# A mixer and mixture-of-experts step on one core: input loads, head order, output projection, router and closing stage rearranged

## The chip, the cores and the metric

The kernel runs on one core of a Trainium2 chip. A core has the matrix engine (PE, with its weight loads listed as PEld), VectorE (DVE), ScalarE (ACT), GpSimd (POOL) and SyncE (SP), and 16 DMA engines. DMAs are issued from the instruction streams of SP, ACT and POOL; the profile lists the issues as SPq, ACTq and POOLq, and the packets by queue: q1 carries what SP issues, q10 what ACT issues, q0 what POOL issues. The metric is the time of one execution in microseconds (us).

## What is computed

One layer for 288 tokens (256 of a prompt, 32 of eight decoded sequences), model width 1024, all in float32:

```
a = rms_norm(x, g_mix);  z = a @ w_in                       # 28 blocks of 128 columns, and r1 with 16
log_a = log_sigmoid(r1 @ w_gk2 + b_gk2) / 16
o1, s1 = chunk_gated_linear(q1, k1, v1, log_a, state)       # 4 heads; chunks of 64 tokens
o2, s2 = chunk_gated_linear(silu(q2), 1-f, silu(i2), log f) # 4 heads
h = x + concat(head_norm(o1)*silu(g1), head_norm(o2)*sigmoid(g2)) @ w_out
logits = rms_norm(h, g_ffn) @ w_router + b_router           # 32 experts, top 4, softmax of the 4
h += sum over the 4 experts of gate * (swiglu(xn @ w_gu[e] + b_gu[e]) @ w_dn[e] + b_dn[e])
h += sigmoid(rms_norm(h, g_ple) @ w_ple_gate) * (p @ w_ple_proj)
y = rms_norm(h, g_final);  outputs: y and the four new states
```

Every expert is computed for up to 64 tokens (its slots); the weights of an expert are 12 MB, of all 32 together 403 MB.

## The kernel before

Activations stand transposed in SBUF: `hT`, `aT` and `acc` are [128, 8, 288], eight chunks of 128 features by 288 tokens. The program is written out by hand for each engine, with semaphores between them; each engine runs its own list in order, and so does each issuing queue.

**Front.** ACT issues `x_prompt` in one DMA and `x_sample`, eight small rows of vectors (L624), `r1w`, `gk2`, `w_rt`, `b_rt`, `p_tok` and `w_pp` before its first copy (L637). PE turns x over (24 transposes, L844) chunk by chunk into PSUM, ACT and DVE copy the even and the odd chunks to `hT`, and DVE multiplies with `g_mix` into `acc`. PE waits for all eight copies, then projects four column blocks from `acc` (the scale 1/rms is applied afterwards); after the first it sums the squares with eight matmuls against `ones`, and between the third and the fourth it computes r1 with eight matmuls of 16 columns out of `aT`. Blocks 4 to 19 follow in a loop, at eight matmuls of 128x128 by 288 each.

**Heads stage.** The last eight column blocks (`project_late`) stand between the parts of the recurrence. Heads go out through PSUM banks `O_BANK`; after heads 0 and 1 come blocks 6 and 7, then heads 2 to 5, the sums of squares of heads 0 to 3 (`head_sums(0)`), heads 6 and 7 and `head_sums(1)`. ACT turns the sums into 1/rms by Ln and Exp (`heads_rinv`), DVE norms each head (`head_norm`, two instructions).

**Output projection.** Eight chunks of `w_out` (512 KB each) go through the same four `wst` slots as `w_in`. Chunks 0 to 3 are computed with heads 0 to 3 first, and then with heads 4 to 7; chunks 4 to 7 follow, each with `stream_chunk(c - 4)`, two accumulating matmuls of 32 columns for the sum of squares and the router's logits. All of the DMAs of `w_out` are on SP, chunks 4 to 7 each after `h_done` of the chunk whose slot they take and ahead of one unit of expert weights.

**Expert weights.** 384 units of 1 MB (`UNITS` = 12 for each expert, eight of `w_gu` with rows of 8 KB and four of `w_dn` with rows of 4 KB) go through 14 slots: 12 of the ring, `vmask` (V_SLOT) and `acc` (A_SLOT). The ring's memory holds the mixer's arrays before. SP issues the first unit after `o_ready` 8 and the first `h_done`, the unit of A_SLOT after `h_done` 8, and every later one when PE has used the unit that held its slot (`u_used`, L516).

**Router.** After the stream chunks PE turns all of `aT` back to rows (24 transposes), then the logits, already multiplied with 1/rms, and the column of 1/rms. DVE finds the top four, counts membership (`memb`), PE ranks tokens within experts by matmuls with a triangle, and turns the gates (`gateT`); DVE builds the one-hot `sel` for four experts at once.

**First expert.** PE gathers the chosen tokens with matmuls of `tok` by `sel`: four chunks, `bias(0)`, then `gate_up` of two chunks, two gathers, `gate_up` of two, two gathers and the rest. One `gate_up` uses one unit in four matmuls of 64 columns by 512, in pairs that share the array.

**Closing stage.** PE computes the per-layer gate in eight chunks (L1302 on), DVE and ACT finish each chunk: scale, sigmoid, multiply, add to `hT`, multiply with `g_final` (`finish`, one chunk behind), squares and their sum (`add_square`); PE turns the finished chunks to rows (`final_chunk`), sums squares to a column (`final_sums`), and the results are scaled and stored.

## Time and profile before

| | us |
|---|---|
| median of three runs | 1249.48 (1248.81 to 1252.28) |
| the profiled execution's own time | 1253.93 |
| span of its trace | 1252.2 |
| PE busy | 1189.8 (95%) |
| DVE busy | 270.5 |
| ACT busy | 183.4 |
| bytes moved | 437.61 MB, mean 349 GB/s |

Times in the trace are counted from the first instruction of the span. A PE that is busy need not be at its peak, and the trace gives the clock that it was granted for each stretch, as a share of full speed.

### The profile page before, as it was taken

The page shows a single profiled execution, that of the slowest core. Times are in us where ns is not written, and L with a number is a line of the kernel's source. Part 1 is how long each engine was busy: PE and PEld are TensorE (multiplying, and loading weights), DVE is VectorE, ACT ScalarE, POOL GpSimd, SP SyncE. Part 2 cuts the span into 40 slices and gives each one's busy share as a digit, 9 for nine tenths or more (in the row PEclk, how much of TensorE's full clock was granted, in tenths as well). Part 3 has the DMA queues.
Part 4 walks back from the last instruction along what each step waited for, and adds up shares of the span by engine and source line. Part 5 has one row for each costly group of instructions (what it writes and reads, how often), then busy time and mean ns, then how long its engine had stood idle before and what let it go on. Part 6 is the DMA issues. An engine that isn't in the chain of part 4 may idle for free.

```text
span 1252.2 us, 12674 instructions
## 1 busy us (share of the span) xinstructions
PE 1189.8 (95%) x5432; PEld 567.6 (45%) x5433; DVE 270.5 (22%) x507; ACT 183.4 (15%) x310; POOL 22.4 (2%) x43
## 2 busy tenths in 40 slices
PE   7999999899999999999999999999999999999887
PEld 4777777643334444444433333333333333333355
DVE  2136733310111112211111111111111111111144
ACT  2142023211010101111110101010101111101032
POOL 3002000000000000000000000000000000000000
PEclk9999979899999999999999999999999999999998
DMA  7462654989999999999999999999999999999931
GB/s 186 118 168 68 163 153 157 380 308 415 418 412 418 417 417 418 417 417 416 418 417 418 417 417 417 416 417 418 417 417 418 417 416 417 417 417 417 417 152 38
DMA packets 127744, 437.61 MB, mean 349 GB/s; under 512 B 9708, under 2 KB 59976, under 8 KB 94888
## 3 DMA queue, kind: packets, MB, share of 16 engines
q1 hardware_dynamic: 123872, 433.22, 87.4%
q10 hardware_dynamic: 3544, 3.30, 0.9%
q8 instruction: 43, 0.70, 0.2%
q0 software_dynamic: 272, 0.28, 0.1%
q14 instruction: 13, 0.11, 0.0%
HBM read 432.04 MB, written 4.72 MB: 349 GB/s over the span
## 4 chain that ended last, share of the span: by engine, by line
PE 51%; DMA 39%; SPq 4%; DVE 3%; ACT 1%; ACTq 1%; issue 1%; DVEq 0%
PE ps L834 49%; DMA ring<-in_w_gu 35%; SPq L516 4%; DMA vmask<-in_w_gu 2%; DMA acc<-in_w_gu 2%; PE ps L1187 1%; ACTq L629 0%; DVE ring L1395 0%; PE ps L1209 0%; ACTq L624 0%; PE ps L1073 0%; DVE wst L1635 0%; DVE wst L1632 0%; DVE ring L1480 0%; PE ps L1291 0%
## 5 line engine op out<-in xcount | busy, mean ns | idle before, releaser
L834 PE MATMUL ps<-ring,s 128*64 128x512 f32 x960 | 215.4, 595 | 13.6 <-DMA ring<-in_w_gu 13.4
L834 PE MATMUL ps<-ring,wst 128*64 128x512 f32 x912 | 207.3, 598 | 2.0 <-ACT wst L769 2.0
L834 PE MATMUL ps<-ring,aT 128*64 128x512 f32 x832 | 187.2, 595 | 7.7 <-DMA ring<-in_w_gu 7.5
L1628 DVE TENSOR_SCALAR wst<-ps 128x512 f32<-128x512 f32 x32 | 22.1, 691 | 741.3 <-PE ps L834 741.3
L834 PEld LDWEIGHTS ps<-ring,s 128*64 128x64 f32 x960 | 66.1, 137 | 160.1 <-issue 115.3
L834 PEld LDWEIGHTS ps<-ring,aT 128*64 128x64 f32 x832 | 57.8, 137 | 131.9 <-issue 104.9
L834 PEld LDWEIGHTS ps<-ring,wst 128*64 128x64 f32 x912 | 61.0, 136 | 115.8 <-issue 112.4
L834 PE MATMUL ps<-aT,wst 128*128 128x288 f32 x384 | 95.1, 408 | 3.0 <-ACT ring L669 3.0
L834 PE MATMUL ps<-sel,tok 128*128 128x256 f32 x384 | 95.4, 388 | 1.2 <-DVE sel L1590 1.2
L767 ACT ACTIVATE wst<-wst 128x512 f32<-128x512 f32 x32 | 20.1, 630 | 506.7 <-DVE wst L1628 506.7
L834 PEld LDWEIGHTS ps<-aT,wst 128*128 128x128 f32 x384 | 72.3, 190 | 25.1 <-ACT ring L669 3.4
L834 PEld LDWEIGHTS ps<-sel,tok 128*128 128x128 f32 x384 | 71.7, 194 | 15.3 <-issue 4.0
L834 PE MATMUL ps<-selT,wst 128*128 128x288 f32 x256 | 72.2, 421 | 2.4 <-issue 1.8
L834 PE MATMUL ps<-acc,wst 128*128 128x288 f32 (+1 forms) x240 | 61.6, 455 | 2.7 <-DVE acc L1507 1.5
L834 PEld LDWEIGHTS ps<-selT,wst 128*128 128x128 f32 x256 | 45.6, 189 | 39.7 <-issue 28.6
L834 PE MATMUL ps<-bgu,ehot 128*64 128x512 f32 x256 | 60.4, 592 | 0.0
L759 ACT COPY wst<-ps 64x512 f32<-64x512 f32 x63 | 36.5, 579 | 128.3 <-PE ps L834 127.5
L834 PEld LDWEIGHTS ps<-acc,wst 128*128 128x128 f32 (+1 forms) x240 | 40.7, 185 | 22.2 <-issue 8.7
L834 PEld LDWEIGHTS ps<-bgu,ehot 128*64 128x64 f32 x256 | 18.3, 137 | 36.3 <-issue 36.3
L834 PE MATMUL ps<-aT,ring 128*128 128x288 f32 x128 | 32.2, 406 | 0.0
L769 ACT COPY wst<-ps 128x512 f32<-128x512 f32 x32 | 18.7, 585 | 84.9 <-PE ps L1187 84.9
L834 PE MATMUL ps<-vmask,aT 128*64 128x512 f32 x112 | 26.6, 595 | 1.1 <-DMA vmask<-in_w_gu 1.1
(253 smaller groups left out, 725.8 us busy)
## 6 DMA issues: line engine op xcount, KB each, us to landing
ring<-in_w_gu SPq DMA_DIRECT2D x224, 1024.0 KB, 20.6
ring<-in_w_dn SPq DMA_DIRECT2D x114, 1024.0 KB, 24.2
vmask<-in_w_gu SPq DMA_DIRECT2D x20, 1024.0 KB, 21.1
wst<-in_w_in SPq DMA_DIRECT2D x28, 512.0 KB, 3.9
acc<-in_w_gu SPq DMA_DIRECT2D x12, 1024.0 KB, 18.1
vmask<-in_w_dn SPq DMA_DIRECT2D x8, 1024.0 KB, 26.0
acc<-in_w_dn SPq DMA_DIRECT2D x6, 1024.0 KB, 23.1
wst<-in_w_out SPq DMA_DIRECT2D x8, 512.0 KB, 3.7
```

The lines of the kernel that those rows point to most:

```text
L516: sp.dma_start(as_unit(weights(e, c), c), unit_src(e, c)).then_inc(u_loaded[slot_of[u]], 16)
L759: act.copy(to[:, half * BANK:(half + 1) * BANK], ps[half * SLOTS:(half + 1) * SLOTS, 5, :]).then_inc(yr_copied, 1)
L767: act.activation(sbuf, gbuf, ACT.Sigmoid, scale=SWIGLU_ALPHA).then_inc(sigm_ready, 1)
L769: act.copy(hidT, ps[:, 3, :]).then_inc(hT_copied, 1)
L834: return pe.matmul(o, lhsT, rhs, start=start, stop=stop, skip_group_check=True)
L1187: ins = pe.transpose(ps[:, 3, c * P:(c + 1) * P], ubuf[:, c * P:(c + 1) * P], ident[:])
L1628: dve.tensor_scalar(gbuf, ps[:, 0, :], SWIGLU_LIMIT, None, ALU.min).then_inc(gate_ready, 1)
```

## The change

x comes in three loads: its first 128 rows on SP ahead of the weights, the second 128 and `x_sample` on ACT. The loads of `r1w`, `gk2`, `w_rt`, `b_rt`, `p_tok` and `w_pp` stand later in ACT's list. PE starts with eight matmuls of the identity, DVE multiplies straight from PSUM, ACT copies all of `hT`, and the squares are summed on DVE so that PE needs one matmul. r1 is computed in four column groups of 32. Heads alternate with the late blocks. The projection of chunk 0 waits head by head. The `w_out` chunks 4 to 7 are issued by ACT, SP starts the expert weights from `su_done` 3 and `o_done` 8 on in another order of slots. Rows are turned back chunk by chunk, the router's logits are multiplied with 1/rms after they are turned, `bias(0)` stands before the ranks, `sel` of the first four experts is built tile by tile, the gates are turned during expert 0. In the closing stage each chunk is finished at once.

```diff
-        queue = [(i, None) for i in range(UNITS + 2)]
+        queue = [(i, None) for i in (V_SLOT, 8, 9, 10, 11, 6, 7, 0, 1, 2, 3, 4, 5, A_SLOT)]
...
+            sp.dma_start(tok[:, 0, :], io["x_prompt"][0, 0:P, :]).then_inc(x0_loaded, 16)
             for i in range(LATE + G):
                 load_cols(i)
...
             sp.wait_ge(su_done, 3)
-            sp.wait_ge(o_ready, HEADS)
-            sp.wait_ge(sp_stored, 16 * 2)
-            sp.wait_ge(s0_stored, 16 * KU)
-            for c in range(UNITS):
-                if c < KD - WSLOTS:
-                    load_cols(NZ + WSLOTS + c)
-                sp.dma_start(unit_dst(c), unit_src(0, c)).then_inc(u_loaded[slot_of[c]], 16)
+            for u in range(UNITS + 2):
                 e, c = u // UNITS, u % UNITS
+                if u == 1:
+                    sp.wait_ge(o_done, HEADS)
+                    sp.wait_ge(sp_stored, 16 * 2)
+                if slot_of[u] == 6:
+                    sp.wait_ge(s0_stored, 16 * KU)
+                if slot_of[u] == 0:
+                    sp.wait_ge(o_ready, HEADS)
+                if slot_of[u] == A_SLOT:
+                    sp.wait_ge(h_done, KD)
+                sp.dma_start(as_unit(weights(e, c), c), unit_src(e, c)).then_inc(u_loaded[slot_of[u]], 16)
...
+            for c in range(KD):
+                act.wait_ge(xg0_ready, c + 1)
+                act.copy(hT[:, c, :], ps[:, c, 0:T]).then_inc(xT_copied, 1)
+                if c == 0:
+                    act.wait_ge(gk2_zeroed, 2)
+                    act.dma_start(r1w[:, :, 0:RANK], io["w_in"][0, :, c_r1:c_r1 + RANK].rearrange("(c p) n -> p c n", p=P)) \
+                        .then_inc(r1w_loaded, 16)
+            for j in range(4):
+                act.dma_start(gk2[j * 32:j * 32 + RANK, :], io["w_gk2"][0]).then_inc(r1w_loaded, 16)
...
+            for c in (0, 4):
+                act.activation(squares[:, c:c + 4, :], hT[:, c:c + 4, :], ACT.Square).then_inc(sq_ready, 1)
+            act.dma_start(w_rt[:], io["w_router"][0].rearrange("(c p) n -> p c n", p=P)).then_inc(small_loaded, 16)
+            act.dma_start(b_rt[:], io["b_router"][0:1, :].to_broadcast([P, E])).then_inc(small_loaded, 16)
...
             for c in range(KD):
                 act.wait_ge(h_ready, c + 1)
                 act.activation(squares[:, c, :], hT[:, c, :], ACT.Square).then_inc(sq_ready, 1)
+                if c + WSLOTS < KD:
+                    act.wait_ge(h_done, c + 1)
+                    act.dma_start(wst[:, (NZ + c) % WSLOTS],
+                                  io["w_out"][0, :, (c + WSLOTS) * P:(c + WSLOTS + 1) * P].rearrange("(c p) n -> p c n", p=P)) \
+                        .then_inc(w_loaded[(NZ + c) % WSLOTS], 16)
...
+            for i in range(8):
+                mm(ps[:, 0, 0:P], ident[:], ident[:], True, True)
...
-                        ins = mm(ps[0:RANK, 7, 0:T], r1w[:, c, :], aT[:, c, :], c == 0, c == KD - 1)
+                        q = slice((c % 4) * 32, (c % 4 + 1) * 32)
+                        ins = mm(ps[q, 7, 0:T], r1w[:, c, :], aT[:, c, :], c < 4, c >= 4)
...
             pe.wait_ge(smp_ready, 1)
             project_late(4, 0)
+            pe.wait_ge(smp_ready, 2)
+            two_heads(0)
             project_late(5, 1)
             pe.wait_ge(su_used, PAIRS)
             state_products(0)
+            two_heads(2)
+            project_late(6, 0)
             state_products(1)
+            two_heads(4)
             head_sums(0)
+            project_late(7, 1)
+            two_heads(6)
             head_sums(1)
...
             def project_out(c, h0, h1):
                 for h in range(h0, h1):
+                    if c == 0:
+                        pe.wait_ge(o_ready, h + 1)
...
             for c in range(4, KD):
                 pe.wait_ge(w_loaded[(NZ + c) % WSLOTS], 16 * (NG + 2))
-                pe.wait_ge(h_ready, c - 3)
+                pe.wait_ge(h_ready, c - 3 if c < 6 else c - 1)
                 project_out(c, 0, HEADS).then_inc(h_done, 1)
-                stream_chunk(c - 4)
+                chunks = range(0 if c == 4 else c - 1, c)
+                for k in chunks:
+                    stream_chunk(k)
+                for k in chunks:
+                    for t in range(TT):
+                        rows_chunk(k, t)
...
+            bias(0)
             pe.wait_ge(memb_ready, 1)
...
-            for c in range(4):
+            for c in range(2):
                 gather_chunk(0, c)
...
-                    if e == 0 and c in (1, 3):
-                        gather_chunk(0, c + 3)
-                        gather_chunk(0, c + 4)
+                    if e == 0 and c in (0, 1, 3):
+                        for k in (2, 3) if c == 0 else (4, 5) if c == 1 else (6, 7):
+                            gather_chunk(0, k)
...
             for c in range(KD):
                 dve.wait_ge(pg_done, c + 1)
                 dve.tensor_tensor(pgt[:, c % 2], ps[:, P_BANK[c], 0:T], rinv[:], ALU.mult).then_inc(pg_scaled, 1)
-                if c:
-                    finish(c - 1)
-                if c > 2:
-                    add_square(c - 2)
-            finish(KD - 1)
-            add_square(KD - 2)
+                if 2 <= c < KD - 1:
+                    add_square(c - 1)
+                finish(c)
```

## Rows read from the trace of the kernel before

**Rows 1.** The page: GB/s moved by DMA, the span in 40 slices of 31.3 us.

```profile
GB/s 186 118 168 68 163 153 157 380 308 415 418 412 418 417 417 418 417 417 416 418 417 418 417 417 417 416 417 418 417 417 418 417 416 417 417 417 417 417 152 38
```

**Rows 2.** Windows: length, PE, PEld, DVE, ACT, POOL busy, clock, DMA share, GB/s.

```profile
250.00:255.00 5.00, 5.00 (x24) 1.90 (x21) 0.00 (x0) 0.00 (x0) 0.00 (x0) 1.00 0.26 74
600.00:1150.00 550.00, 525.57 (x2371) 205.85 (x2367) 80.52 (x133) 58.05 (x103) 0.00 (x0) 1.00 1.02 417
```

**Rows 3.** Timeline (start, us, what): first gather, first down unit, last gate unit.

```profile
241.38 7.57 PE L834 MATMUL ps<-sel,tok 128*128 128x256 f32 x24 [1.19 <-DVE sel L1590]
...
248.88 1.94 PE L834 MATMUL ps<-bgu,ehot 128*64 128x512 f32 x8
...
275.15 0.20 PEld L834 LDWEIGHTS ps<-ring,wst 128*64 128x64 f32 x4 [0.33 <-issue]
...
1184.36 0.20 PEld L834 LDWEIGHTS ps<-ring,s 128*64 128x64 f32 x4 [1.44 <-DMA ring<-in_w_gu]
```

**Rows 4.** Timeline of the front.

```profile
7.01 5.27 ACTq L629 DMA_DIRECT2D b_rt<-in_b_router  x1
...
7.98 6.92 PE L844 MATMUL ps<-ident,tok 128*128 128x128 f32 x24 [7.98 <-DMA tok<-in_x_sample]
...
16.45 6.11 PE L834 MATMUL ps<-acc,wst 128*128 128x288 f32 x16 [1.28 <-ACT hT L637]
...
34.13 4.05 PE L834 MATMUL ps<-aT,r1w 128*16 128x288 f32 x16
...
43.36 17.00 PE L834 MATMUL ps<-aT,wst 128*128 128x288 f32 x69
```

**Rows 5.** Queues from 5 to 6 us: packets, MB, share of 16 engines.

```profile
q10 hardware_dynamic: 88, 0.36, 88.0%
q1 hardware_dynamic: 90, 0.05, 15.4%
```

**Rows 6.** Queue q1 from 7 to 8 us, and from 212 to 214 us.

```profile
q1 hardware_dynamic: 490, 0.24, 115.4%
...
q1 hardware_dynamic: 129, 0.82, 100.0%
```

**Rows 7.** Heads stage: the timeline of SP and PE, and one window.

```profile
176.63 3.92 SPq L490 DMA_DIRECT2D out<-ring  x4
...
182.59 4.19 PE L834 MATMUL ps<-ring,ones 128*128 128x288 f32 x8
...
190.74 2.19 PE L834 MATMUL ps<-ring,ones 128*128 128x288 f32 x8
...
175.00:177.00 2.00, 2.00 (x9) 1.05 (x5) 1.08 (x2) 0.00 (x0) 0.00 (x0) 0.50 0.00 0
```

**Rows 8.** Timeline of the output projection and its first and last addition.

```profile
194.38 19.67 PE L834 MATMUL ps<-acc,wst 128*128 128x288 f32 x80 [1.46 <-DVE acc L1507]
...
204.45 0.45 DVE L1537 TENSOR_TENSOR hT<-hT,ps 128x288 f32<-128x288 f32 x1 [3.86 <-PE ps L834]
...
223.96 4.15 PE L834 MATMUL ps<-acc,wst 128*128 128x288 f32 x16
...
228.14 0.45 DVE L1537 TENSOR_TENSOR hT<-hT,ps 128x288 f32<-128x288 f32 x1 [3.83 <-PE ps L834]
```

**Rows 9.** Timeline of the router, and the clock in one window of it.

```profile
236.01 0.80 DVE L1565 TENSOR_REDUCE memb<-selg 128x96 f32<-128x384 f32 x1
...
240.00:245.00 5.00, 3.81 (x11) 2.99 (x11) 2.19 (x5) 0.39 (x1) 0.00 (x0) 0.50 1.03 419
```

**Rows 10.** Timeline of the end: last chunk scaled, last sum, its Ln.

```profile
1240.04 0.46 DVE L1715 TENSOR_TENSOR wst<-ps,rinv 128x288 f32<-128x288 f32 x1 [2.02 <-PE ps L834]
...
1243.90 1.42 PE L834 MATMUL ps<-ones,tok 128*128 128x1 f32 x12 [1.65 <-DVE tok L1710]
...
1245.36 0.26 ACT L814 ACTIVATE rcol<-ps,eps 128x2 f32<-128x2 f32 x1 [0.59 <-PE ps L834]
```

**Rows 11.** The page: DMA issues of w_out, count, KB, median us from issue to landing.

```profile
wst<-in_w_out SPq DMA_DIRECT2D x8, 512.0 KB, 3.7
```

More of the change, by code:

```diff
@@ L181, in build @@
         reset = sb("reset", [P, T])
+        lgs = reset[0:E, :]
         maskf = ring[:, BLOCKS * SLOTS:BLOCKS * SLOTS + P + 32]
@@ L445, in _ @@
             cols = [(io["w_in"], c0 + j * P) for c0 in group_cols for j in range(G)]
-            cols += [(io["w_out"], j * P) for j in range(KD)]
+            cols += [(io["w_out"], j * P) for j in range(WSLOTS)]
             def load_cols(i):
@@ L550, in _ @@
             lk.add(pool.memset(ones[:], 1.0))
+            lk.wait()
+            pool.affine_select(out=ident[:], in_=ident[:], compare_op=ALU.not_equal, fill=1.0, base=0,
+                               pattern=[[-1, P]], channel_multiplier=1).then_inc(consts_ready, 1)
+            pool.affine_select(out=upper[:], in_=ones[:], compare_op=ALU.is_gt, fill=0.0, base=0,
+                               pattern=[[1, P]], channel_multiplier=-1).then_inc(consts_ready, 1)
+            pool.memset(gk2[:], 0.0).then_inc(gk2_zeroed, 1)
+            pool.memset(r1w[:], 0.0).then_inc(gk2_zeroed, 1)
             lk.add(pool.memset(reset[:], 1.0))
@@ L1087, in _, with bias @@
-            rinv_columns(1)
+            pe.wait_ge(rinv_ready, 2)
+            for t, (t0, n) in enumerate(tiles):
+                ins = pe.transpose(ps[0:n, 0, t * P:t * P + E], rinv[0:E, t0:t0 + n], ident[0:E, 0:E])
+            ins.then_inc(rc_done, 1)
+            def bias(e):
+                pe.wait_ge(ehot_ready, e + 1)
+                for b in range(2):
+                    halves(b, ehot[:], bgu[:, b * FF:b * FF + BANK], bgu[:, b * FF + BANK:(b + 1) * FF], True, False)
+            pe.wait_ge(bdn_loaded, 16)
@@ L1149, in combine_half @@
                         ins.then_inc(cb_done, 1)
-            def bias(e):
-                pe.wait_ge(ehot_ready, e + 1)
-                for b in range(2):
-                    halves(b, ehot[:], bgu[:, b * FF:b * FF + BANK], bgu[:, b * FF + BANK:(b + 1) * FF], True, False)
             def gate_up(e, c):
@@ L1571, in _ @@
             lk.add(dve.tensor_tensor(pk[:], pk[:], psum_k[:, :, 1:2].to_broadcast([P, NT, TOPK]), ALU.mult))
+            dve.wait_ge(rank_done, 1)
+            for t, (t0, n) in enumerate(tiles):
+                lk.add(dve.scalar_tensor_tensor(rankp[0:n, t, :], ps[0:n, RANK_BANK, t * E:(t + 1) * E], 1.0, memb[0:n, t, :],
+                                                ALU.add, ALU.mult))
             lk.wait()
+            for t in range(NT):
+                dve.tensor_tensor(sel[:, t], iota1[:, 0:SLOTS].unsqueeze(1).to_broadcast([P, QUAD, SLOTS]),
+                                  rankp[:, t, 0:QUAD].unsqueeze(2).to_broadcast([P, QUAD, SLOTS]),
+                                  ALU.is_equal).then_inc(sel_ready, 1)
+            lk.add(dve.tensor_copy(cnt_f[:, 0:E], ps[0:1, RANK_BANK, NT * E:(NT + 1) * E]))
+            lk.wait()
+            lk.add(dve.tensor_reduce(cnt_f[:, E:E + 1], cnt_f[:, 0:E], AX_X, ALU.max))
+            lk.wait()
+            dve.tensor_copy(cnt_i[:], cnt_f[:]).then_inc(cnt_ready, 1)
             lk.add(dve.tensor_tensor(gated.rearrange("p t k e -> p (t k) e"), onehot.rearrange("p t k e -> p (t k) e"),
```

338 lines of the change are left out of this document (162 added, 176 removed).

## The prediction

> **What bounds the kernel now.** I read the row of GB/s on the page first: from slice 10 to slice 38 it stands at 417 or so [rows 1], and the windows say the same for 600 to 1150 us, while PE is busy for 525.57 of those 550 us [rows 2]. One unit of 1.0486 MB at 417 GB/s is 2.51 us, an expert of twelve 30.2 us; PE needs 30.2 x 525.57/550 = 28.8 us for one. So DMA sets the pace of the expert stage, and at its end PE waits for the last gate unit of expert 31, at 1184.4 [rows 3]. From there to the end of the span are 67.8 us.
>
> Then I asked when that stream began to run without a gap. In 250 to 255 it moves only 74 GB/s [rows 2]: all 14 slots are full and wait for PE's first use. A unit 14 places later can be issued only when PE lets a slot go. The first gate unit is let go about 252.6 (the bias matmuls end at 250.8 [rows 3], and it takes 1.8 us itself), the first down unit, number 8, about 277.1. Counting 2.51 us a place, these ask for a stream that starts at 252.6 and at 277.1 - 8 x 2.51 = 257.0; later units ask for less, as PE gains 1.4 us an expert. The reader is to see that the time when PE uses **the first down unit** (275.15 [rows 3]) moves the end one to one, that loading the first 14 units sooner by itself moves nothing, and that beyond it only the closing stage counts.
>
> **Front.** PE is in the loop at 43.36 and started its first projection at 16.45, for ACT's copies; ACT came to them only after its DMA issues, b_rt's alone 5.27 us [rows 4]. With x and the vectors first I put the start at 12: PE had all of x at 7.98 and took 6.92 us for its 24 transposes [rows 4]; a third of them now run before the last load, and the copies no longer follow them. Bounds 9 and 16.4. That is -4.4. Summing the squares takes eight matmuls as r1 does, 4.05 us [rows 4]; one is left, 0.5: -3.5. r1 in four column groups runs two rounds of 0.5 in place of 4.05: -3.0, bound -2.0. PE then waits for the squares' sum and the norm, which come from ACT and DVE, some 0.9; if b_rt's issue holds ACT again for 5.27, up to 4.6. The queue is emptier by then, as r1w is long through, so I take 0.9. **Front: -10.0**, bounds -6.3 and -13. The Trainium skill ("TensorE: Matmul & The Clock Gate", Part 3, Measured speedup vs the span model) gives three column tiles a speedup of 2.38, not four; by that r1 would take 1.7 us and the sum be 0.7 us smaller. No row of this kernel shows four groups.
>
> **Heads.** PE does the same work in another order. From 175 to 177 the granted clock was 0.50, the level of 1.2 GHz, and the same four sums took 4.19 us there and 2.19 later [rows 7]; that level lasted from 174 to 187, and the work in it took 5.1 us more than its like elsewhere. PE was not idle; thin matmuls in a row came before it. With a 3.9 us block between every two heads I expect the clock to hold: -5.1, bound 0. The norms of heads 0 to 3 are made while block 7 and heads 6, 7 run, so the wait of 1.46 [rows 8] goes, and 1.5 us of small gaps. **Heads: -8.1**, bounds -3 and -8.1. The projection starts at 194.4 - 18.1 = 176.3; its first half costs 7.7 us, heads 4 to 7 are normed in time to within 0.2, so the first addition is at 186.3 for 204.45 [rows 8].
>
> **The w_out loads of chunks 4 to 7.** This is the step that decides. They are now issued by ACT (q10) while SP's expert weights fill q1. Two queues at once took turns: 88 packets of 4 KB in q10 and 90 of 512 bytes in q1 in the same us [rows 5], one for one, whatever their size; a pair takes an engine 16/88 = 0.18 us. A w_out load is 1024 packets of 512 bytes, 64 an engine. A packet of w_gu has 8 KB: some 98 in 2 us (0.80 of the 0.82 MB) [rows 6], 0.32 us each, so a pair is 0.335. SP gets to the weights thus: the w_out load of chunk 3 waits for block 7 and, with the four stores of states behind it (3.9 us of issues [rows 7]), is issued from 171 to 175. 2.6 MB in 512-byte packets at 0.24 MB a us [rows 6] would last to 183; I take 182. Chunk 4's load starts at 188.6 (addition 0.45, square 0.44, issue, and 1.5 us to the first byte: the 0.37 MB of 250 to 255 [rows 2] are 0.9 us of flow, after a release at 252.6). Of the eight w_gu units 2.6 are through, 5.4 are left: 43 packets an engine. Chunk 4 takes 43 x 0.335 + 21 x 0.18 = 18.2 us, landing at 207. Chunk 5 pairs with 43 packets of w_dn (7.8), with the 8 of unit 12 (2.7), and goes alone for the rest: about 217.7. Chunks 6 and 7 follow at 2.2 us each, since unit 13 waits for `h_done` 8. PE was through with chunk 3 at 191.9, so it stands for 15 us; then chunk 4 at a fallen clock 5.7 (16 records took 6.11 at the start [rows 4], 4.15 later [rows 8]), streams and transposes 3, a wait to 217.7, chunks of 3.9 with 0.75 between. The last addition comes at 230.9 for 228.14 [rows 8]: **+20.9**, and what front and heads won is gone. From below the loads cost about 4 (the shorter pair for a queue nearly empty), from above they end when q1 runs dry, near 213 for chunk 4. The Trainium skill ("DMA: Bandwidth & Descriptors", Queues, rings and completion order) says that an engine drains a packet of some 9 to 17 descriptors from one queue before it turns to the next; by that chunk 4 would need 4 to 7 turns and as many descriptors of the weights, the same within 2 us. Its section Issuing engines are not separate DMA queues says that a second issuer saves only issue time, which speaks against this part.
>
> **Router.** Stream chunks 4 to 6 and 16 row transposes are done before the last addition, the logits don't wait for 1/rms: lg_done 3.1 earlier against the last addition. `memb` by two additions saves 0.25 of the 0.80 [rows 9], the per-tile `sel` 0.6, the gates' transposes leave the path, but `bias(0)` and the scaling by a column cost it some 0.8. **-3.1**, bounds -1 and -5.
>
> **First expert.** The bias matmuls (1.94 [rows 3]) leave the stretch, the wait for the first copied gather costs 0.9, and gathers ran at half clock until 245 [rows 3, 9], 2 us lost; bias(0) in DVE's stretch keeps PE at work. -2.8, bounds 0 and -3.5. So the first down unit comes at 275.15 - 18.1 + 20.9 - 3.1 - 2.8 = 272.
>
> **Closing.** PE's eight chunks are as long. After the last one DVE scaled at 1240.04, then finished two chunks, and the Ln of the sums came at 1245.36 after 1.42 us of twelve records [rows 10]. Now one chunk is finished, its three sums take 0.4, but ACT loads its table after the last square: Ln at 1243.7, -1.6. The wait for the first finished chunk goes: -0.5. **-2.1**, bounds -1 and -2.5.
>
> The sum is -18.1 + 20.9 - 3.1 - 2.8 - 2.1 = -5.2: 1253.9 becomes 1248.7 for the profiled execution, 4.4 above the median of 1249.5, which becomes 1244.3.
>
> **The rivals.** (a) ACT's loads are not held up: engines read ahead, and the small packets slip in; chunk 4 costs 4 us. For it: the shares from 5 to 6 and from 7 to 8 us sum to over 100% [rows 5, 6], so packets overlap. Against it: the counts, 88 to 90. The last addition is then at 212 + 1, and the sum -5.2 - 17 = -22: 1227. (b) Nothing comes of it: the clock also falls among the new heads (+5.1), or b_rt holds ACT (+3.7), with no other change: 1249. Against it: heads are shorter stretches now. (c) Slower: PE's clock stays at 0.50 when it comes back from the 15 us without work, through chunks, streams and transposes to the gathers, as it was at 0.50 in 240 to 245 [rows 9], when DVE had kept it waiting for the router. Some 30 us of work at half speed cost 15, less 4 counted: +11, so 1255. It decides from 5.2 us lost, 10 us of work beyond what I count. Against it: the first projection, which also came after a rest, lost only 2 us to it (6.11 for 4.15 [rows 4, 8]).
>
> **How the numbers follow.** 0.3% of 1249.5 is 3.75 us, about what a measurement can tell. The main case gets 0.58, its own range 1240 to 1249 from the bounds of front, router and the first expert; (a) 0.26, and between 1223 and 1238; (b) 0.10; (c) 0.06. Faster: 0.70 of the main case, all of (a), a little of (b): 0.69. Same 0.21, slower 0.10. The range 1226 to 1250 leaves out the ends of (a), (c) and the tails, 2 in 10.
>
> **What would show it.** The loop at 33 in place of 43; clock 1.00 through the heads; PE idle for 10 us or more ahead of chunk 4 of the projection with the wait on w_out, and a landing time of some 18 us for 512 KB on ACT's queue in place of 3.7 [rows 11]; the first down unit at 272; Ln some 3.7 us after the last chunk is scaled, for 5.3. I am wrong if the wait at chunk 4 is under 6 us (rival a), or if the end does not follow the first down unit.

## The result and the profile after

The changed kernel takes 1259.26 us (median of 4, 1258.41 to 1259.78), the kernel before beside it 1250.11 us. The ratio is 1.0071, with a 95% interval of 1.0053 to 1.0088: the change makes the kernel slower by 0.7%. I had forecast 1244 and given "slower" one chance in ten. The profiled execution took 1258.41 us, with a span of 1256.6 us. Of all executions in this document one, of b_heads, is set apart as slow (1385.79 us at a mean granted clock of 0.846 for 0.989 to 0.993); it counts in no ratio.

The timeline of the changed kernel, from the loop to the last addition (start, us, what). The number behind x counts records; a matmul of the program gives two of them, of two instructions each:

```profile
34.41 2.83 PE L851 MATMUL ps<-aT,wst 128*128 128x288 f32 x11
...
179.19 15.68 PE L851 MATMUL ps<-acc,wst 128*128 128x288 f32 x64
...
189.16 0.45 DVE L1592 TENSOR_TENSOR hT<-hT,ps 128x288 f32<-128x288 f32 x1 [0.76 <-PE ps L851]
...
211.01 6.08 PE L851 MATMUL ps<-acc,wst 128*128 128x288 f32 x16 [16.14 <-DMA wst<-in_w_out]
...
223.17 4.15 PE L851 MATMUL ps<-acc,wst 128*128 128x288 f32 x16 [2.99 <-DMA wst<-in_w_out]
...
232.99 4.05 PE L851 MATMUL ps<-acc,wst 128*128 128x288 f32 x16
...
237.07 0.45 DVE L1592 TENSOR_TENSOR hT<-hT,ps 128x288 f32<-128x288 f32 x1 [4.00 <-PE ps L851]
```

PE is in the loop 8.95 us sooner than in [rows 4] and starts the out projection 15.2 us sooner than in [rows 8]. Then it stands for 16.14 us ahead of chunk 4 and for 2.99 us ahead of chunk 5, each time for a w_out load, and the last addition comes 8.9 us *later* than in [rows 8]. The cause stands in three views. First, ACT's own issues of these loads:

```profile
189.65 0.39 ACTq L750 DMA_DIRECT2D wst<-in_w_out  x1
191.52 0.38 ACTq L750 DMA_DIRECT2D wst<-in_w_out  x1
193.46 13.39 ACTq L750 DMA_DIRECT2D wst<-in_w_out  x1
206.92 11.93 ACTq L750 DMA_DIRECT2D wst<-in_w_out  x1
```

The third and fourth issue block ACT for 13.39 and 11.93 us. Second, the landing times (count, KB, median us from issue to landing), 26.2 us on ACT's queue where SP's loads of the same size take 3.8:

```profile
wst<-in_w_out SPq DMA_DIRECT2D x4, 512.0 KB, 3.8
wst<-in_w_out ACTq DMA_DIRECT2D x4, 512.0 KB, 26.2
```

Third, the two queues from 194 to 196 us (units in packets of 8 KB) and from 206 to 208 us (4 KB): packets, MB, share of 16 engines. q1 carries the expert units, q10 the w_out loads:

```profile
q1 hardware_dynamic: 97, 0.79, 92.9%
q10 hardware_dynamic: 97, 0.05, 8.2%
...
q1 hardware_dynamic: 183, 0.69, 88.1%
q10 hardware_dynamic: 184, 0.09, 16.6%
```

The counts are equal and the bytes are not: a packet of 512 bytes goes for each one of 8 or of 4 KB. In each us from 194 to 217 the two counts differ by 5 at most. While PE stands its clock falls; the first window below covers the heads, the two others the stand (the last three columns are granted clock, DMA share and GB/s):

```profile
174.00:187.00 13.00, 13.00 (x67) 10.65 (x66) 4.50 (x11) 7.65 (x10) 0.00 (x0) 1.00 0.97 313
195.00:201.00 6.00, 0.00 (x0) 0.00 (x0) 0.73 (x2) 0.00 (x0) 0.00 (x0) 0.74 1.03 419
201.00:211.00 10.00, 0.00 (x0) 0.00 (x0) 0.00 (x0) 0.44 (x1) 0.00 (x0) 0.50 1.03 394
```

So chunk 4 takes 6.08 us for 4.15. From the router to the end: the first gather, the first down unit (of `w_dn`), the last gate unit (of `w_gu`), the last combine (the sixteen records that bring the last expert's rows back to the tokens, here in two pieces), the gate chunks of the closing stage, the last chunk scaled and its Ln:

```profile
246.89 2.83 PE L851 MATMUL ps<-sel,tok 128*128 128x256 f32 x12 [1.02 <-DVE sel L1639]
...
277.99 2.37 PE L851 MATMUL ps<-ring,wst 128*64 128x512 f32 x10
...
1187.62 1.94 PE L851 MATMUL ps<-ring,s 128*64 128x512 f32 x8 [0.54 <-DMA ring<-in_w_gu]
...
1203.52 1.97 PE L851 MATMUL ps<-lnbuf,wst 128*128 128x288 f32 x7 [0.68 <-ACT wst L778]
1208.58 3.84 PE L851 MATMUL ps<-lnbuf,wst 128*128 128x288 f32 x9 [3.10 <-issue]
1212.26 4.53 PE L851 MATMUL ps<-aT,ring 128*128 128x288 f32 x18
...
1246.44 0.46 DVE L1771 TENSOR_TENSOR wst<-ps,rinv 128x288 f32<-128x288 f32 x1 [1.89 <-PE ps L851]
...
1250.15 0.26 ACT L833 ACTIVATE rcol<-ps,eps 128x2 f32<-128x2 f32 x1
```

The first down unit is 2.8 us later than in [rows 3] and the last gate unit 3.3 us: the end of the stream follows the first down unit, as the prediction's first part has it. Longer than before is the stand in the last combine, 3.10 us in which PE waits for nothing that the profile names ("issue"), and the nine records behind it are slow (3.84 us, where at full clock a record is 0.25). In the kernel before this stand is 1.75 us long and comes after twelve records:

```profile
1200.26 3.18 PE L834 MATMUL ps<-selT,wst 128*128 128x288 f32 x12 [0.68 <-ACT wst L759]
1205.19 1.13 PE L834 MATMUL ps<-selT,wst 128*128 128x288 f32 x4 [1.75 <-issue]
```

### The profile page after: what moved, and what is told of

Same layout as the page of the kernel before. It is cut to its first block, busy times and chain, and to the rows that moved or that the text cites. A ratio compares the mean times of both kernels' runs of the same rounds, so it can differ in the third digit from the quotient of the medians.

```text
span 1256.6 us, 12703 instructions
## 1 busy us (share of the span) xinstructions
PE 1183.8 (94%) x5440; PEld 564.4 (45%) x5441; DVE 273.5 (22%) x508; ACT 184.8 (15%) x314; POOL 22.9 (2%) x45
## 4 chain that ended last, share of the span: by engine, by line
PE 49%; DMA 42%; SPq 3%; DVE 3%; ACT 1%; issue 1%; ACTq 0%; DVEq 0%
PE ps L851 47%; DMA ring<-in_w_gu 35%; SPq L519 3%; DMA wst<-in_w_out 3%; DMA vmask<-in_w_gu 2%; DMA acc<-in_w_gu 2%; PE ps L1238 1%; PE ps L864 0%; DMA vec_rows<-in_gn_hgrn 0%; DVE ring L1444 0%; PE ps L1260 0%; ACTq L636 0%; DVE wst L1688 0%; DVE wst L1691 0%; DVE ring L1529 0%
## 5 line engine op out<-in xcount | busy, mean ns | idle before, releaser
L786 ACT ACTIVATE wst<-wst 128x512 f32<-128x512 f32 x32 | 20.2, 631 | 507.0 <-DVE wst L1684 507.0
L851 PEld LDWEIGHTS ps<-aT,wst 128*128 128x128 f32 x384 | 73.4, 193 | 24.6 <-ACT ring L685 3.4
L851 PE MATMUL ps<-lnbuf,wst 128*128 128x288 f32 x256 | 73.6, 428 | 3.8 <-issue 3.1
L851 PEld LDWEIGHTS ps<-sel,tok 128*128 128x128 f32 x384 | 70.1, 190 | 14.5 <-issue 5.1
L851 PEld LDWEIGHTS ps<-lnbuf,wst 128*128 128x128 f32 x256 | 46.5, 193 | 41.6 <-issue 30.0
L851 PEld LDWEIGHTS ps<-aT,ring 128*128 128x128 f32 x128 | 24.0, 190 | 6.3
## 6 DMA issues: line engine op xcount, KB each, us to landing
vmask<-in_w_gu SPq DMA_DIRECT2D x20, 1024.0 KB, 20.2
acc<-in_w_gu SPq DMA_DIRECT2D x12, 1024.0 KB, 18.2
acc<-in_w_dn SPq DMA_DIRECT2D x6, 1024.0 KB, 24.6
```

The costliest lines, as they stand in the source:

```text
L786: act.activation(sbuf, gbuf, ACT.Sigmoid, scale=SWIGLU_ALPHA).then_inc(sigm_ready, 1)
L851: return pe.matmul(o, lhsT, rhs, start=start, stop=stop, skip_group_check=True)
```

## The experiments

Every time below is a median; "ratio" is to the kernel before, run beside it, with its 95% interval.

**The kernel before, once more.** No edit.

> The kernel before, once more. Its first profiled execution took 1253.93 us, 4 us over its median, and had a half-clock stretch from 174 to 187 us in the heads; I had taken 5.1 us off for it. Theory A (that stretch is a rare guest, so its 5.1 us were never in the median): the new profile has clock 1.00 from 174 to 187, the out projection starts near 189 instead of 194.4, and the span is near 1248. Rival B (the stretch belongs to the kernel): clock 0.50 there again and the projection at 194 to 195; then the 4 us between profile and median lie elsewhere, and the heads gain of the change is real. Beside itself the kernel should come out within 0.3%, which also tells how far a comparison of this kernel can be trusted.

It took 1250.52 us beside 1248.23, ratio 1.0013 (1.0001 to 1.0026). Windows of the heads stage and of the out projection, and the projection's start:

```profile
174.00:187.00 13.00, 13.00 (x93) 10.97 (x92) 2.48 (x4) 8.10 (x13) 0.00 (x0) 1.00 0.71 203
...
200.00:240.00 40.00, 35.79 (x180) 25.14 (x179) 14.38 (x47) 9.55 (x18) 1.90 (x2) 0.92 0.98 373
...
190.97 6.33 PE L834 MATMUL ps<-acc,wst 128*128 128x288 f32 x25 [1.86 <-DVE acc L1507]
```

The clock is 1.00 from 174 to 187, the projection starts 3.4 us sooner than in [rows 8], and the span is 1248.9 us for 1252.2. Theory A holds. From the loop to the projection PE takes 146.6 us for 151.0, so the stretch at half clock cost 4.4 us and not 5.1, and it reached the loop 1 us later in this execution, so the start is 191 and not 189. The profiles of b_front, b_wout and b_pad12 below have the old order of heads too, clock 1.00 in that stage, and 145.1 to 146.7 us for the same way: one profile of five has the stretch. The mean clock of each execution goes with its time: the profiled one of the prediction had 0.988 at 1253.93 us, this one 0.993 at 1250.63; beside b_front the kernel before took 1246.58 us at 0.994 and 1254.57 at 0.986. As far as these figures tell, the spread of this kernel's times is stretches of half clock that come in some executions and not in others. The interval, just above 1 for a kernel beside itself, says that 0.1% tells nothing here.

**The w_out loads back on SP.**

```
 (SP)  for u in range(UNITS + 2):
           ...
+          if 1 <= u <= KD - WSLOTS:
+              sp.wait_ge(h_done, u)
+              sp.dma_start(wst[:, (NZ + u - 1) % WSLOTS], <w_out, chunk u + 3>)
 (ACT) -   act.wait_ge(h_done, c + 1); act.dma_start(wst[...], <w_out, chunk c + 4>)
```

> The changed kernel, but the w_out loads of chunks 4 to 7 are issued by SP again, in turn with the expert units 1 to 4, each after its h_done, as in the kernel before. Theory Q (the loads lost their time to the units queued on the other queue): chunk 4 lands some 4 to 6 us after its issue instead of 15 to 30, PE waits under 3 us ahead of chunks 4 and 5, the last addition comes near 214 instead of 237.1, the first down unit near 255 to 257, and the end follows it by 20 to 23 us: 1237 to 1240. Rival S (the stream's start sets the end, and units issued 10 us later than in the changed kernel cost it back): first down unit early, but the last gate unit not before 1180, and 1248 to 1255.

1236.47 us (1236.41 to 1236.62), ratio 0.9903 (0.9883 to 0.9923): theory Q, half a us below its range. The page gives 3.8 us to landing for all eight loads. Projection, chunk 7 of it, first down unit and last gate unit:

```profile
179.07 19.56 PE L851 MATMUL ps<-acc,wst 128*128 128x288 f32 x80
...
211.28 4.05 PE L851 MATMUL ps<-acc,wst 128*128 128x288 f32 x16
...
256.27 7.09 PE L851 MATMUL ps<-ring,wst 128*64 128x512 f32 x32
...
1165.68 1.94 PE L851 MATMUL ps<-ring,s 128*64 128x512 f32 x8 [0.55 <-DMA ring<-in_w_gu]
```

Chunk 4 follows chunk 3 without a gap. Chunk 7 starts 32.2 us after the projection did, for 53.8 in the changed kernel: the loads' place on ACT's queue costs 21.6 us there. The first down unit comes 21.7 us sooner and the span is 21.9 us shorter. The expert units from the second on start 8.5 us later here (189.46 for 180.98), and nothing is lost by it: rival S is out.

**ACT issues, but SP waits for its loads.**

```
 (SP)  if u == 1:
           ...
+          for k in range(WSLOTS):
+              sp.wait_ge(w_loaded[(NZ + k) % WSLOTS], 16 * (NG + 2))
```

> The changed kernel with ACT still issuing the w_out loads of chunks 4 to 7, but SP holds unit 1 and all later ones until those four loads have landed. Theory Q (sharing between the queues is the cost): as good as with the loads on SP, since 14 units need only 35 us and are not wanted before 252: last addition near 214, 1237 to 1240. Rival I (what costs is that ACT issues them, between its squares: 13.4 and 11.9 us of blocked issues): the issues stay long, the squares and so the streams stay late, and the time stays above 1250.

1236.68 us, ratio 0.9908 (0.9886 to 0.9929), the same as with the loads on SP. Queue q10 from 194 to 196 us, with no row of q1 in that window, and the landing time on ACT's queue:

```profile
q10 hardware_dynamic: 980, 0.49, 83.9%
...
wst<-in_w_out ACTq DMA_DIRECT2D x4, 512.0 KB, 4.1
```

The four issues take ACT 0.37 to 0.39 us each. So the blocked issues of the changed kernel were not a property of ACT; they come where its queue drains slowly (a_split below, in between, has 3.81 and 7.53 us). Rival I is out: the company on the DMA engines is the cost, not the issuer. The second unit and all behind it start at 200.27 here, 19.3 us later than in the changed kernel, and that too costs nothing.

**Smaller packets for the units.** Units 1 to 13 in four loads of 512 columns (w_dn: 256), nothing else.

```
 (SP)  for q in range(4):
           sp.dma_start(<quarter q of the unit's columns>).then_inc(u_loaded[slot_of[u]], 16)
       # waits on u_loaded of these slots: + 48
```

> The changed kernel, all its queues and its order kept; only units 1 to 13 are loaded in four parts of 512 columns each, so that their packets have 2 KB instead of 8 KB or 4 KB. Theory Q1 (packets are taken one for one from the two queues, whatever their size): a pair of packets then moves 2.5 KB instead of 8.5 KB, 0.10 us instead of 0.34, and chunk 4 of w_out (64 packets an engine) lands after some 6 to 9 us instead of 20; chunk 5 follows 4 to 7 us later; the last addition near 220, 1240 to 1245. Rival Q2 (bytes are shared, or the older queue is drained first): the units carry as many bytes as before, chunk 4 lands as late as before (PE at it at 211), and the time stays within 2 us of 1259.

1246.15 us (1244.46 to 1249.3), ratio 0.998 (0.9967 to 0.9994): 13 us less than the changed kernel with the same bytes in the same queues, though 1.2 us above the slow edge of what Q1 had given. From 198 to 200 us (units in 2 KB) and from 216 to 218 us (1 KB):

```profile
q1 hardware_dynamic: 309, 0.57, 79.7%
q10 hardware_dynamic: 308, 0.16, 28.4%
...
q1 hardware_dynamic: 442, 0.43, 71.0%
q10 hardware_dynamic: 441, 0.22, 41.6%
```

The counts stay equal at four packet sizes, 8, 4, 2 and 1 KB, and the w_out load gets 0.05, 0.09, 0.16 and 0.22 MB in 2 us; the median landing is 18.9 us for 26.2. That is the mechanism, shown by dose. PE starts chunk 4 at 204.69, 11.9 us after the issue of its load for the 6 to 9 expected. The first packet of w_out came only some 3.5 us after its issue (192.82 to about 196), as it did in the changed kernel (189.65 to 193); with q1 empty in a_hold it came within 1.5 us (189.49 to between 190 and 191). So the first packet comes some 2 us later beside a full queue; no run shows why. The profiled execution (1247.96 us) also started the projection 3.2 us later than the changed kernel, with a mean clock of 0.83 from 80 to 100 us, which the edit does not touch. The Trainium skill ("DMA: Bandwidth & Descriptors", Queues, rings and completion order) lets an engine drain 9 to 17 descriptors of one queue before it turns to the next; no window here shows such turns, not even those of 1 us in the changed kernel, in which each queue moves three to six packets an engine, and the measured counts decide: one for one.

**The third part alone, on the kernel before** (slot order, early units, w_out of chunks 4 to 7 on ACT).

> The kernel before with the third part alone: the new order of the slots, units 1 to 12 from the last head on, w_out of chunks 4 to 7 issued by ACT. By packets taken one for one: the heads end at 188, the first of these loads is issued near 201.5, when some 6 of the 13 queued units are through; 64 packets an engine of 512 bytes then pair with 16 of 8 KB (0.335 us) and 48 of 4 KB (0.18): chunk 4 lands near 218, chunk 5 near 225, last addition near 239 instead of 224.7, so +15: 1262 to 1266. Rival K (a cost that comes with the ACT queue whatever is queued in the other): the 22.8 us that the loads cost in the changed kernel, 1271. Rival B (the earlier start of the units gives something back): under 1258.

1264.49 us, ratio 1.0123 (1.0099 to 1.0146), inside the 1262 to 1266 that packets one for one had given. PE starts chunk 4 at 215.59 after a stand of 12.04 us and the last chunk at 232.25, so that the last addition is near 236.4; both come some 2.5 us sooner than written. The cost is 14 us here and near 22 in the changed kernel. The first of these loads is issued 14.5 us after the second unit here (198.33, 183.85) and 8.7 us after it there (189.65, 180.98), so more of the queued units are through.

**The front alone.**

> The kernel before with the front of the changed one alone: x in three loads, eight warm-up matmuls, copies after DVE's scaling, one matmul for the sum of the squares, r1 in four column groups, the small loads behind the squares. Theory F (the front's gain goes to the end one to one): PE in the loop at 34.4 instead of 43.4, first down unit 9 us sooner, and 1239 to 1241 beside 1248 to 1250. Rival W (the loop and the stages behind it wait for the w_in loads or for DVE, which do not come sooner): the loop starts at 34 but the out projection comes less than 5 us sooner, 1244 or later.

1242.14 us beside 1250.66, ratio 0.9937 (0.9915 to 0.9959), a gain of 7.9 by the ratio. Loop at 35.0, projection at 181.7, first down unit at 262.24, 8.5 us before the one of e_before: theory F. The span is 7.6 us shorter; of the 0.9 us between, the closing stage took back 0.6 (69.3 us for 68.7, see below). The median is 1.1 us above the range expected.

**The heads alone.** The order of the late projections and heads, as in the change.

> The kernel before with the new order of the heads stage alone: a block of the late projection between every two heads, norms of heads 0 to 3 made early, waits of the first out projection by head. Theory D (my 5.1 us for a fallen clock stood only in the one profiled execution): against the second profile of the kernel before, where the clock held, the out projection starts 2.8 us sooner, at 188, and the median gains 2 to 3.5: 1245 to 1247. Rival C (the clock does fall in the usual run of the kernel before and the new order prevents it): 6 to 8 us, 1240 to 1243. Rival N (nothing): within 1 us.

1250.29 us beside 1250.66, ratio 0.9994 (0.9979 to 1.0009): no gain, rival N, though its profile has the projection 4.4 us sooner than e_before (186.60) and the first down unit 3.0 us sooner (267.73). The last gate unit is 3.2 us sooner too, and the span 0.5. Between the last two stands the last combine: PE stood after 10 records for 2.36 us where the kernel before stands after 12 for 1.8, and six records at half clock took 3.04 us. Nothing of the closing stage had been edited. That called for a theory of its own.

**Where PE stands in the last combine.** Between the last expert and the last combine PE jumps over a branch of some 300 instructions, which would serve experts with more rows than slots. A first try, 40 no-ops in that branch:

> The changed kernel with the w_out loads on SP, and 40 no-ops added for PE inside the branch that is jumped over (more rows than slots), so that the code behind it is 40 instructions further on; nothing that runs is changed. In every profile PE stands once among the sixteen matmul records of the last combine without waiting for anything (issue): 1.8 us after 12 of them in the kernel before, 2.9 to 3.1 after 7 in the changed one, followed by half clock for the other nine. Theory X (PE runs out of code at a fixed place of the program, which the change moved five records forward): the stand is gone from there or comes elsewhere, the last gate unit to the end of the span shrinks by 2 to 3 us from 69.0, and 1233.5 to 1235. Rival Y (the place hangs on the jump or on data loads, not on where the code lies): the stand stays after 7 records, 1236.5 as before.

1236.73 us, stand after 7 records for 2.87 us. It tests nothing: the compiler had dropped the no-ops, PE's program was as long as before. It stands as a repeat of a_wout_sp in another comparison (0.9902 for 0.9903). Then matmuls in the same place, which never run but do stay in the program:

```
+ def pad(n):
+     for _ in range(3):                       # 16 in a_padmm
+         mm(ps[:, 0, 0:P], ident[:], ident[:], True, True)
- overflow_blocks(pe, most, extra_block)
+ overflow_blocks(pe, most, extra_block, pad)
```

> The kernel before with three matmuls more for PE at the end of the branch that is jumped over; they never run, but the code behind them lies 12 instructions further on. (The 40 no-ops tried before were dropped by the compiler, so that run was a repeat.) In the compiled programs the last combine begins at instruction 10701 in the kernel before, 10705 with the new heads, 10706 with the new front, 10711 in the changed kernel, and PE stands after 12, 10, 10 and 7 matmul records of two instructions each: always at 10725. Theory X (PE has its code up to a fixed place, and the next piece comes at a fixed time after the jump): here the combine begins at 10713, the stand comes after 6 records, some 2.9 us long, and the rest runs at half clock; 2 to 3 us more from the last gate unit to the end: 1251 to 1253. Rival Y (the place hangs on what runs, not on where the code lies): after 12 records as before, and no change.

> As the changed kernel with the w_out loads on SP, with 16 matmuls (64 instructions) more at the end of the branch that is jumped over: the last combine begins at 10775, beyond 10725. Theory X: the jump leads past all the code that PE has; it stands right at the jump with none of the 16 records done, and goes on at the same time after it as in the other kernels, some 5.8 us, then with all 16 ahead of it: 1238 to 1240. If instead the fetch starts at the jump's target and comes sooner than 5.8 us, it is 1235 to 1237.

b_pad12 took 1254.54 us beside 1250.86, ratio 1.0023 (1.0009 to 1.0037), with nothing changed that runs. Its ten executions lie apart, three at 1250.5 to 1250.7 and seven at 1253.5 to 1255.8; the profile is one of the seven. The combine in b_pad12, then in a_padmm (1243.09 us, ratio 0.9942, 0.9924 to 0.9961):

```profile
1197.46 1.72 PE L834 MATMUL ps<-selT,wst 128*128 128x288 f32 x6 [0.68 <-ACT wst L759]
1202.33 4.27 PE L834 MATMUL ps<-selT,wst 128*128 128x288 f32 x10 [3.15 <-issue]
```

```profile
1192.98 5.58 PE L851 MATMUL ps<-lnbuf,wst 128*128 128x288 f32 x16 [5.80 <-issue]
```

Six records before the stand as forecast, and none at all with the longer pad. b_pad12 lost 2.9 us by the ratio, 3.7 by the medians, which is above the 1251 to 1253 expected. In the profiles it is 3.0 us from the last gate unit to the first gate chunk (24.9 for 21.9). The low end of its interval, 1.0009, is under the 1.0013 that the kernel before gave beside itself, so that the place of the stand is shown, and the price in the usual execution less well. a_padmm came 3 to 5 us above its expectation. Its stand was as expected and its last gate unit to the end 1.8 us longer than in a_wout_sp, but the first down unit came at 262.64 for 256.27: 1.8 us were lost before the loop, 2.9 between loop and projection (mean clock 0.94 from 60 to 120 us for 1.00) and 1.7 in the first gather. Why these stretches ran slower is open. Two kernels take the other way, a loop of one warm-up matmul in place of eight written out, and PE's branch left out:

> The changed kernel with the w_out loads on SP, and the eight warm-up matmuls of the front written as a loop of one: 23 instructions fewer, the last combine begins at 10688. Theory X: all 16 records of the combine lie ahead of 10725, PE stands behind them at the head of the gate chunks or not at all, nothing of the combine runs at half clock, and the time from the last gate unit to the end shrinks by 2.5 to 4 us: 1232.5 to 1234. Rival Y: the stand stays after 7 records, 1236.5.

> As the changed kernel with the w_out loads on SP, but PE's part of the branch for experts with more rows than slots is left out, with its jump (the inputs here never take it; the other engines keep theirs). Theory X (the jump over some 310 instructions is what leaves PE without code): no stand in the last combine, half clock nowhere near it, and 3 to 5 us less from the last gate unit to the end: 1231.5 to 1233.5. Rival Z (the code fetch is late because the loads of w_ple_gate fill the queues): the stand stays, with or without a jump.

a_short took 1235.34 us (1233.6 to 1237.41), ratio 0.9884 (0.9863 to 0.9905), 1.3 us above the range of theory X and by its interval not told apart from a_wout_sp; a_nobranch 1233.45, ratio 0.9867 (0.985 to 0.9883), as expected. In a_short the sixteen records run in one piece and the gate chunks follow at once:

```profile
1183.68 4.15 PE L851 MATMUL ps<-lnbuf,wst 128*128 128x288 f32 x16 [0.68 <-ACT wst L778]
1187.66 8.12 PE L851 MATMUL ps<-aT,ring 128*128 128x288 f32 x32
```

a_nobranch has 0.83 us of issue ahead of the combine and none in it, so rival Z (late for the loads of w_ple_gate) is out. What a_short wins behind the last gate unit, 4.6 us, shows in its median only in part: in its profile the first gather took 4.46 us for the 2.83 of a_wout_sp, at a mean clock of 0.67 from 226 to 231, and the first down unit came 2.4 us later. The table puts the profiles side by side; the place is counted in the compiled programs, "resumes" is from the start of the last down unit to the end of the stand, worked out from the timelines:

| kernel | combine begins at instruction | records before the stand | stand, us | resumes, us | last gate unit to the end, us |
|---|---|---|---|---|---|
| a_short | 10688 | 16 | none | | 64.4 |
| a_warm3 | 10691 | 16 | 0.23 | | 64.7 |
| b_heads2 | 10699 | 13 | 1.43 | 7.46 | 68.9 |
| before, second profile | 10701 | 12 | 1.83 | 7.62 | 68.7 |
| b_heads | 10705 | 10 | 2.36 | 7.66 | 71.4 |
| b_front | 10706 | 10 | 2.25 | 7.55 | 69.3 |
| after | 10711 | 7 | 3.10 | 7.68 | 69.0 |
| a_wout_sp | 10711 | 7 | 2.88 | 7.46 | 69.0 |
| b_pad12 | 10713 | 6 | 3.15 | 7.48 | 72.2 |
| a_padmm | 10775 | 0 | 5.80 | 7.74 | 70.8 |

A record is two instructions, so the stand comes at about 10725 in every kernel, and the time at which PE goes on is the same to 0.3 us. Queue q8 (instruction) moves one packet of 0.02 MB some 1.5 to 3 us before PE goes on. In a_short that packet comes between 1186 and 1187, while PE is still at records that it has; a_nobranch has none from 1176 to 1191, and 42 in all for 43. The Trainium skill ("Runtime: NRT & Kernel Launch", Instruction fetch mechanics) says that code comes in blocks of 16 KiB, fetched in sequence, and that a jump out of the blocks at hand has to wait for its target. The trace agrees on the block (q8: 0.70 MB in 43 packets). By the table the jump's target was at hand here in all kernels but a_padmm, since PE ran six records or more behind it, and what it stood for lay behind 10725; the price is the work that lies behind that border plus the clock that falls meanwhile.

**Two more, for what was still open.** b_heads2 is b_heads without PE's waits on `o_copied` between heads; a_warm3 is a_wout_sp with `range(3)` warm-up matmuls for `range(8)`.

> As b_heads (the kernel before with the new order of the heads stage alone), without PE's waits on o_copied between the heads, which its waits on osq_ready cover: six instructions fewer, so the last combine begins at 10699 instead of 10705. Theory X (the heads' 3 us were given back by the moved stand): the stand comes after 13 records, the time from the last gate unit to the end is 68.7 or less instead of 71.4, the first down unit again near 267.7, and the median 1246 to 1248. Rival H (the new heads are worth nothing in the usual run, the 3.0 us of the profile were chance): within 1 us of the kernel before.

> The changed kernel with the w_out loads on SP and three warm-up matmuls instead of eight: 20 instructions fewer, the last combine begins at 10691. Theory X: its 16 records lie ahead of 10725, and the time from the last gate unit to the end is 64 to 65 us as in a_short instead of 69.0; five warm-ups less cost nothing, since the last of them ends when x lands: 1232 to 1234. Rival W (the warm-up keeps PE's clock up in the front): the front comes out 1 us or more later, 1234.5 to 1236.

b_heads2 took 1248.52 us beside 1250.02, ratio 0.999 (0.9977 to 1.0002). The stand came after 13 records, as forecast, the first down unit at 267.93, and 68.9 us from the last gate unit to the end. The span of the profile was 2.5 us under that of e_before, the median 1.5 us under the kernel beside it. That lies between theory X and rival H and within what can be measured: the moved stand explains the loss of b_heads in its profile, but how much the new heads gain in the usual run stays between 0 and 3 us. In the profiles the way from the loop to the projection is 143.2 us in both for 146.6 in e_before.

a_warm3 took **1233.48 us** (1232.82 to 1235.94), ratio 0.986 (0.9841 to 0.9879): the fastest version that still has all of the computation. It beats the kernel before by 1.4% and the changed one by 2%, with two small edits to the change. It is not told apart from a_nobranch. Its profile is the slowest of its four executions, 1235.94 us: 4.3 us shorter than a_wout_sp from the last gate unit to the end, but 3.3 us later at the first down unit, half of it again in the first gather (4.51 us). Rival W stays open: the loop starts at 35.89, as in a_wout_sp (35.98), but a_pad40, the same program as a_wout_sp, has it at 34.77. So the 3 us between the medians of a_wout_sp and a_warm3 may not be the moved stand alone.

## Why the prediction was wrong

The mechanism that it called decisive was right, and so were the places: equal packet counts, the stand at chunk 4, the clock falling in it, the end that follows the first down unit, Ln 3.7 us after the last chunk is scaled (1246.44 to 1250.15). The step that failed first is the last one of the sum, "4.4 above the median of 1249.5, which becomes 1244.3", on top of a heads term of which 5.1 us were the same half clock. Two terms were mis-sized besides: the w_out loads, +20.9 for a measured +24.1, and the closing stage, -2.1 for +1.1, whose stand behind the jump the sum left out. Term by term, measured between the two profiles:

| term | forecast | measured | from |
|---|---|---|---|
| front | -10.0 | -9.0 | loop, 43.36 to 34.41 |
| heads | -8.1 | -6.2 | projection, 194.38 to 179.19, less the front |
| w_out loads | +20.9 | +24.1 | last addition +8.9, less the 15.2 won before it |
| router | -3.1 | -3.4 | last addition to first gather, 13.2 to 9.8 |
| first expert | -2.8 | -2.7 | gather to first down unit, 33.8 to 31.1 |
| stream | 0 | +0.4 | first down unit to last gate unit |
| closing | -2.1 | +1.1 | last gate unit to the end, 67.84 to 68.98 |
| profiled execution | -5.2 | +4.4 | spans, 1252.2 to 1256.6 |
| its place against the median | -4.4 | +0.9 | 1253.93 to 1249.5; 1258.41 to 1259.26 |

The rows differ by 9.6 us and the last one by 5.3, together the 15 us between 1244.3 and 1259.3. The front came near its -10.0 in part by luck: the projection started at 14.24 and not at 12, and from there to the loop it took 20.2 us for 26.9, 1.1 us better than counted.

**The heads' clock was counted twice.** Of the -8.1, 5.1 us stood for the half clock from 174 to 187 [rows 7]. The same profiled execution lay 4.4 us above the median, and I took that off too. e_before shows that both are for the most part one thing: without that stretch the span was 3.3 us shorter, and the kernel's times go with their mean clock. Against the median the heads could give 3 us (8.1 less 5.1), and b_heads and b_heads2 gave 0.4 and 1.5. This error alone is about 5 us, and without it the same sum says 1249, "no change".

**The w_out loads cost 3.2 us more.** The pair of packets was sized rightly: chunk 4 was due 18.2 us after its first packet and came after 17 to 18 (between 193 and 194, to 211.01). That is luck in part: the packets of 8 KB ended at 204, when 36 packets of w_out an engine had gone beside them and not 43. What was missing is the lag of the first packet, some 3.4 us after the issue (189.65) for the 1.5 us counted. In all, chunk 4 started 31.8 us after the projection for 30.7, chunk 5 came 12.2 us behind it for 10.7, and the rest is behind that. The "some 18 us" from issue to landing was 21.4 to PE's start for chunk 4 and 26.2 in the median of the four, which stand behind each other in one queue. Against a_wout_sp the place on ACT's queue costs 22.8 us by the medians; 2.5 of the 24.1 us are transposes and sums moved ahead of the last addition, which the router then gives back.

**The closing stage lost 3.2 us against the forecast.** The part that I forecast is there: from the first gate chunk to the end 44.3 us for 46.1, -1.7 for -2.1. But between the last gate unit and that chunk it takes 24.6 us for 21.8, since the change made PE's program ahead of the combine 10 instructions longer. No row that I had read spoke of it, though the stand of 1.75 us was in the trace of before; I had taken it for a constant. b_pad12, a_short and a_padmm show it to be none: as the stand comes sooner in the combine, more records are left behind it, nine for four here, and they ran at half clock.

Router, first expert and the one-to-one rule for the first down unit held within 0.4 us. Rival (a) is excluded by the counts; a_hold shows what it would have been worth. Rival (c) was half right: the clock fell to 0.50, but came back with chunk 4 (mean 0.63 from 212 to 216, then 1.00), so that it cost 2 us and not 15. The kernel was slower by another way than the one I had given for it. The 6.11 us of the first projection in [rows 4], from which I had the price of a fallen clock, stand where the row of the clock reads 1.00:

```profile
18.00:20.00 2.00, 2.00 (x6) 1.37 (x5) 0.23 (x2) 1.90 (x2) 0.00 (x0) 1.00 0.93 371
```

Six records began in these 2 us and ten from 22 to 24, with 1.00 in the row both times. So the row does not show every slow stretch at the start of an execution, and mean clocks are to be compared with care; chunk 4 at 6.08 us, with 0.50 in the row, bears the price out. I had also taken the Trainium skill's three-tile speedup as a caution for r1 ("TensorE: Matmul & The Clock Gate", Part 3, Measured speedup vs the span model, 2.38); in four column groups its sixteen records took 1.18 us for 4.05, 3.4 times faster, close to the 1.0 that the sum used.

## What to carry to other kernels

A small load that someone waits for does not belong beside a deep queue of large packets: both queues advance packet by packet, so 512 KB in packets of 512 bytes took 26 us next to packets of 8 KB and 4 us alone. Issue it ahead of them in the same queue or hold them back; that the units then started 8.5 or 19.3 us later cost nothing here. Before a forecast is moved from a profiled execution to a median, ask what made that execution slow, and don't bank the same stretch again as a gain. And where an engine jumps over a long branch, the length of the program ahead of it is part of the timing: compare the stand behind the jump in both traces before an effect is put down to the edit.

## What was not expected of the hardware

- Twelve instructions that never run cost some 3 us (1.0023, 1.0009 to 1.0037; 3.0 in the profile), and with 20 fewer, five warm-up matmuls, the median fell by 3 us (1236.47 to 1233.48) and the way from the last gate unit to the end by 4.3. The stand lies at one fixed place of the program and ends 7.5 to 7.7 us after the last down unit starts.
- A queue that drains slowly holds its issuer for long: 13.39 and 11.93 us in one instruction of ACT, 0.37 with the other queue held back.
- A stand of 2.87 us or more in the combine was followed by half clock in every profile that had it, one of 1.83 us or less in none, and of the two in between (2.25 and 2.36 us) the second was.
